# A decoder trunk on one core: the MLP up projection as its own stage with seven block products, its result through DRAM

## What is computed

```
for i in range(2):
    x = x + mixer_i(rmsnorm(x, norm_mix[i]))
    h = rmsnorm(x, norm_mlp[i])                       # (1024, 1024)
    x = x + square(relu(h @ w_up[i])) @ w_down[i]      # w_up (1024, 4096), w_down (4096, 1024)
```

## Time and profile before

| what | value |
|---|---|
| median of 3 runs | 2750.98 us (2746.82 to 2753.17) |
| the profiled execution | 2752.24 us, span of its trace 2750.4 us |
| PE busy | 2658.4 us (97%), 12273 matmuls |
| DVE busy | 1572.6 us (57%) |
| ACT busy | 746.5 us (27%) |
| POOL busy | 477.9 us (17%) |
| DMA | 146.67 MB, mean 53 GB/s |

### The profile page before, as it was taken

One profiled execution on the slowest core, in us unless ns is written; L12 is line 12 of the kernel. 1 busy time (PEld: TensorE's weight loads), 2 busy tenths in 40 slices (PEclk: granted clock), 3 DMA queues, 4 the chain that ended last, 5 costly groups with the idle time before them and its releaser, 6 DMA issues.

```text
span 2750.4 us, 35656 instructions
## 1 busy us (share of the span) xinstructions
PE 2658.4 (97%) x12273; PEld 2216.8 (81%) x12273; DVE 1572.6 (57%) x3049; ACT 746.5 (27%) x1400; POOL 477.9 (17%) x473
## 2 busy tenths in 40 slices
PE   8999999999999999999999988999979999999999
PEld 6878878788788788888888877888868888888887
DVE  7554454544677644544445488888875444454443
ACT  6232222322313211111111255555551111111112
POOL 2102011020001211111111153323331111111010
PEclk9999999999999999999999999999999999999999
DMA  6012120121432111111111101001011111111111
GB/s 201 27 47 69 47 74 12 47 65 51 149 97 87 39 54 46 46 46 48 59 46 46 38 23 39 17 24 39 32 31 46 46 46 60 46 46 46 46 46 61
DMA packets 124795, 146.67 MB, mean 53 GB/s; under 512 B 15729, under 2 KB 97937, under 8 KB 124690
## 3 DMA queue, kind: packets, MB, share of 16 engines
q1 hardware_dynamic: 122386, 141.14, 16.4%
q10 hardware_dynamic: 2304, 4.20, 0.4%
HBM read 128.54 MB, written 16.78 MB: 53 GB/s over the span
## 4 chain that ended last, share of the span: by engine, by line
PE 80%; DVE 11%; issue 5%; ACT 3%; POOL 0%; DVEq 0%; DMA 0%; ACTq 0%; SPq 0%; POOLq 0%
PE ps L420 26%; PE ps L422 26%; PE ps L421 25%; ACT xn L1460 1%; DVE xT L597 1%; DVE hT_lo L465 1%; DVE wqg_lo L387 1%; DVE smax L1507 1%; PE ps L858 1%; DVE pT_lo L1484 1%; PE ps L859 1%; PE ps L860 1%; DVE hss L1540 1%; PE ps L906 0%; PE ps L890 0%
## 5 line engine op out<-in xcount | busy, mean ns | idle before, releaser
L597 DVE TENSOR_TENSOR xT<-ps,xT 128x512 f32<-128x512 f32 x704 | 475.0, 689 | 273.7 <-PE ps L422 273.7
L420 PE MATMUL ps<-aT_hi,wd_hi 128*128 128x512 f32 x1408 | 555.2, 394 | 7.9 <-DVE xT L597 4.9
L421 PE MATMUL ps<-aT_lo,wd_hi 128*128 128x512 f32 x1408 | 550.3, 391 | 0.0
L422 PE MATMUL ps<-aT_hi,wd_lo 128*128 128x512 f32 x1408 | 550.2, 391 | 0.0
L420 PE MATMUL ps<-hT_hi,wu_hi 128*128 128x512 f32 x1024 | 401.1, 392 | 0.0
L422 PE MATMUL ps<-hT_hi,wu_lo 128*128 128x512 f32 x1024 | 399.1, 390 | 0.0
L421 PE MATMUL ps<-hT_lo,wu_hi 128*128 128x512 f32 x1024 | 399.1, 390 | 0.0
L694 POOL TENSOR_TENSOR sqr_t<-relu_t 128x512 f32<-128x512 f32 x128 | 188.1, 1470 | 1168.8 <-DVE relu_t L702 1168.8
L420 PEld LDWEIGHTS ps<-aT_hi,wd_hi 128*128 128x128 f32 x1408 | 265.8, 189 | 63.3 <-DVE xT L597 5.8
L422 PEld LDWEIGHTS ps<-aT_hi,wd_lo 128*128 128x128 f32 x1408 | 265.7, 189 | 55.9
L421 PEld LDWEIGHTS ps<-aT_lo,wd_hi 128*128 128x128 f32 x1408 | 266.0, 189 | 53.8
(11 more groups left out here) (255 smaller groups left out, 4333.4 us busy)
## 6 DMA issues: line engine op xcount, KB each, us to landing
raw<-in_w_up SPq DMA_DIRECT2D x64, 512.0 KB, 3.9
raw<-in_w_down SPq DMA_DIRECT2D x64, 512.0 KB, 3.3
raw<-in_ret_w_in SPq DMA_DIRECT2D x48, 512.0 KB, 4.7
y_dram<-xn SPq DMA_DIRECT2D x32, 256.0 KB, 2.3
raw<-y_dram SPq DMA_DIRECT2D x16, 512.0 KB, 3.2
raw<-in_ret_w_out SPq DMA_DIRECT2D x16, 512.0 KB, 3.4
xtok<-in_x SPq DMA_DIRECT2D x8, 512.0 KB, 5.9
xT<-x_dram SPq DMA_DIRECT2D x8, 512.0 KB, 7.5
```

The lines of the kernel that those rows point to most:

```text
L420: pe.matmul(bank, ah, bh, start=(i == 0), stop=False)
L421: pe.matmul(bank, ah, bl, start=False, stop=False)
L422: last = pe.matmul(bank, al, bh, start=False, stop=(i == len(pairs) - 1))
L597: dve.tensor_tensor(xT[:, k, cols], ps[:, banks[m % len(banks)], :], xT[:, k, cols], ALU.add).then_inc(x_add, 1)
```

## The change

The up projection is taken out of the groups. It becomes a stage of its own over 8 pairs of groups (512 hidden features each). In a pair the product is one of 2x2 blocks: the weights are split by the two halves of K and by two halves of the features, the activations by the two halves of K and the two halves of the tokens. Strassen's scheme in Winograd's form makes it of seven block products (numbered 1 to 7) in place of eight. With two feature tiles (q = 0, 1) a pair is 14 products of 4 x 3 = 12 matmuls, called steps 0 to 13 here. The seven activation operands `bh`/`bl` are made once a layer; the sums of weights (`u_sum`, 8 a pair) are made for each pair. Results are gathered in PSUM and in SBUF slots (`u_copy_act`, 6 a pair, and `u_add_dve`, 8 a pair), get their relu times `rb` (DVE, in place), their square (ACT, in place), and go to `a_dram` (8 stores of 256 KB). The first pair (`first=True`) has its own order of products, and its weight sums are POOL's. `xT` is saved to `x_dram` before the stage and read back at its end, since the operands take its room. The down projection then runs over the 16 groups as before, but reads `a` from DRAM in two pieces of 512 KB a group, split by ACT and DVE like weights. The norm before the MLP is done for both halves at once.

```diff
+ORDER = {True: (1, 2, 5, 6, 4, 7, 3), False: (1, 6, 4, 7, 2, 5, 3)}
+RESULTS = {True: ((11, 0), (11, 1), (22, 0), (21, 0), (22, 1), (21, 1), (12, 0), (12, 1)),
+           False: ((21, 0), (21, 1), (11, 0), (11, 1), (22, 0), (22, 1), (12, 0), (12, 1))}
+U_BANK = {1: 4, 6: 4, 7: 4, 2: 0, 5: 2, 3: 2, 4: 6}
...
+        def u_load_next(sp, layer, p, first):
+            g = PAIRS * layer + p
+            for j in range(4):
+                sp.wait_ge(u_lo, OPS * g + op_pos(first, 7 if j < 2 else 3, j % 2) + 1)
+                u_load(sp, layer, p + 1, j)
...
+        def u_sum(eng, layer, p, first, i, q):
+            g = PAIRS * layer + p
+            done = lambda k: eng.wait_ge(s_set, 8 * g + SUM_AT[first][k, q])
+            if i == 5:
+                arrived(eng, PC_U[layer], p, 4, q)
+                arrived(eng, PC_U[layer], p, 4, 2 + q)
+                wait(eng, u_lo, OPS * g)
+                eng.tensor_tensor(us1[:, q, :, :], weight(7, q), weight(4, q), ALU.add).then_inc(s_set, 1)
+            if i == 7:
+                done(5)
+                eng.tensor_tensor(weight(7, q), weight(1, q), weight(7, q), ALU.subtract).then_inc(s_set, 1)
+            if i == 6:
+                done(5)
+                wait(eng, s_set, 8 * g)
+                eng.tensor_tensor(us2[:, q, :, :], us1[:, q, :, :], weight(1, q), ALU.subtract).then_inc(s_set, 1)
...
+        def u_pe(pe, layer, p, first, between=lambda s: None):
+            for s in range(OPS):
...
+                if i == 6:
+                    pe.wait_ge(u_cp, 6 * g + 1 + q)
+                if i == 7:
+                    pe.wait_ge(u_cp, 6 * g + 3 + q)
+                if i == 3:
+                    pe.wait_ge(u_add, 8 * g + c_pos(first, 22, q) + 1)
+                product(pe, ps[:, U_BANK[i] + q, :],
...
                          bh[i][:, k, :], bl[i][:, k, :]) for k in range(4)], begin=i in (1, 2, 4, 5)).then_inc(u_mm, 1)
+                between(s)
...
+        def u_dve(dve, layer, p, ahead):
+            for s in range(OPS):
+                for c, q in results_of(s):
+                    u_add_dve(dve, layer, p, False, c, q)
+                if s + URING < OPS:
+                    if s + URING >= OPS - 2:
+                        u_sum(dve, layer, p, False, 3, s % 2 ^ 1)
+                    u_lo_dve(dve, layer, p, False, s + URING)
+                else:
+                    ahead(s)
+                for c, q in results_of(s):
+                    u_relu_dve(dve, layer, p, False, c, q)
...
+        def next_lo(dve, layer, p, s):
+            j = s + URING - OPS
+            if j in (2, 3):
+                for i in (5, 7, 6):
+                    u_sum(dve, layer, p + 1, False, i, j - 2)
+            u_lo_dve(dve, layer, p + 1, False, j)
...
+        def edge_dve(dve, layer, final):
+            for i in (0, 1):
+                u_lo_dve(dve, layer, 0, True, 4 + i)
+            for kk in range(4):
+                t_dve(dve, layer, 6, kk, final)
+            for kk in range(4):
+                b_lo_dve(dve, layer, 6, kk)
+            norm_rstd(dve, 2 * layer + 1, 0)
+            dve.wait_ge(n_rsq, RSQ * (RS_AT[2 * layer + 1] + 1))
+            for half in range(2):
+                norm_dg(dve, 2 * layer + 1, half)
+            (u_lo 6, 7; t_dve 4 x4; t_dve 7 x4; b_lo_dve 3 x4; b_lo_dve 4 x4; u_lo 8, 9; b_lo_dve 7 x4; u_lo 10, 11)
+            (u_add_dve 11 x2; u_relu_dve 11 x2; u_lo 12, 13)
+            for s in (7, 8, 9):
+                next_lo(dve, layer, 0, s)
+            for s in (10, 11):
+                for c in (22, 21):
+                    u_add_dve(dve, layer, 0, True, c, s - 10)
+                next_lo(dve, layer, 0, s)
+                for c in (22, 21):
+                    u_relu_dve(dve, layer, 0, True, c, s - 10)
...
+        def first_pair_pool(pool, layer, final):
+            pool.wait_ge(down_mm, final + TILES)
+            for q in range(2):
                u_sum(pool, layer, 0, True, 5, q)
            for q in range(2):
                u_sum(pool, layer, 0, True, 7, q)
                u_sum(pool, layer, 0, True, 6, q)
            for q in range(2):
                u_sum(pool, layer, 0, True, 3, q)
...
+            def between(s):
+                if s == 1:
+                    norm_stat_pe(pe, n, 0)
+                    pe.wait_ge(x_add, final + TILES)
+                if s == 3:
+                    for half in range(2):
+                        norm_rb_pe(pe, n, half)
...
+        def up_sp(sp, layer, final):
+            for m in range(TILES):
+                x_save(sp, m, final)
+            for c, q in RESULTS[True][:2]:
+                u_store(sp, layer, 0, True, c, q)
+            u_load_next(sp, layer, 0, True)
...
+            for kind in ("m1", "u2", "u3", "e"):
+                for q in range(2):
+                    sp.wait_ge(a_out[kind, q], 16 * PAIRS * (layer + 1))
...
+        def dn_dve(dve, layer, g, b):
+            for m in range(TILES):
+                if isinstance(g, int) and g == 0 and m < KT:
+                    dve.wait_ge(x_in_s[m], 16 * (3 + layer))
+                add(dve, DG_D[layer] + g, m)
+                if m % 4 == 0:
+                    dn_lo_dve(dve, layer, g + 1, m // 4, b)
```

More of the change, by code:

```diff
@@ L368, in load_piece @@
         def load_piece(sp, m0, i, per, j, src, fold):
-            wait(sp, w_lo, m0 + per * i + j - RING + 1)
+            wait(sp, w_lo, wc(m0) + per * i + j - RING + 1)
             apart(sp)
@@ new lines, in u_store, with weight @@
+        def u_store(sp, layer, p, first, c, q):
+            g = PAIRS * layer + p
+            kind = keep_of(first, c)
+            sp.wait_ge(u_sq, 8 * g + c_pos(first, c, q) + 1)
+            apart(sp)
+            half = c % 10 - 1
+            sp.dma_start(a_dram[bass.ds((4 * p + 2 * q + c // 10 - 1) * P, P), half * HALF:(half + 1) * HALF],
+                         keep(kind, q)).then_inc(a_out[kind, q], 16)
+        def weight(i, q):
+            k0 = raw[:, q, :].rearrange("p (k n) -> p k n", n=256)
+            k1 = raw[:, 2 + q, :].rearrange("p (k n) -> p k n", n=256)
+            return {1: k0[:, :, 0:P], 7: k0[:, :, P:2 * P], 2: k1[:, :, 0:P], 3: k1[:, :, 0:P], 4: k1[:, :, P:2 * P],
+                    5: us1[:, q, :, :], 6: us2[:, q, :, :]}[i]
@@ new lines, in u_hi_act @@
+        def u_hi_act(act, layer, p, first, s):
+            i, q = op_at(first, s)
+            g = PAIRS * layer + p
+            wait(act, u_mm, OPS * g + s - URING + 1)
+            if i in (1, 2, 4):
+                arrived(act, PC_U[layer], p, 4, q if i == 1 else 2 + q)
+            else:
+                act.wait_ge(s_set, 8 * g + SUM_AT[first][i, q])
+            if layer == 1 and first and s == 5:
+                act.wait_ge(n_ss, sums(3, 1, KT - 1))
+            act.activation(uw_hi[:, s % URING, :].rearrange("p (k n) -> p k n", n=P), weight(i, q),
+                           ACT.Copy).then_inc(u_hi, 1)
@@ new lines, in down_act @@
+        def down_act(act, layer, after):
+            for j in range(4):
+                dn_hi_act(act, layer, 1, j, 1)
+            after()
+            with act.Fori(1, MLP_GROUPS // 2) as gg:
+                for b in range(2):
+                    for j in range(4):
+                        dn_hi_act(act, layer, 2 * gg + b, j, D_BUF[b])
+        def dn_dve(dve, layer, g, b):
[5 more added lines that the diff above has]
+                    dn_lo_dve(dve, layer, g + 1, m // 4, b)
@@ new lines, in down_dve, with down_sp @@
+        def down_dve(dve, layer, last_adds):
+            dn_dve(dve, layer, 0, 1)
+            with dve.Fori(0, MLP_GROUPS // 2 - 1) as gg:
+                dn_dve(dve, layer, 2 * gg + 1, 2)
+                dn_dve(dve, layer, 2 * gg + 2, 1)
+            last_adds()
+        def down_sp(sp, layer):
+            for j in range(4):
+                dn_load(sp, layer, 1, j)
+            with sp.Fori(2, MLP_GROUPS) as g:
+                for j in range(4):
+                    dn_load(sp, layer, g, j)
```

963 lines of the change are left out of this document (610 added, 353 removed).

## The result

The changed kernel took 2784.41 us (median of four runs, 2783.64 to 2784.62) against 2752.07 us (2746.82 to 2753.94) for the kernel before on the same chip: a ratio of 1.0119, 95% interval 1.0103 to 1.0135. It is slower by 32 us; the forecast was 2752, the range 2716 to 2776. The profiled run's span is 2781.6 us against 2750.4.

A forecast was written before the change was run, and what follows sets the result against it. It took TensorE (97% busy) and its matmul count as the bound. From a profiled 2752.24 us, -87.0 + 27.6 + 46.1 + 11.6 + 2.4 = +0.7 us; adjusted to the median, it forecast 2752, range 2716 to 2776.

The forecast's parts named there:

- saving of 87 us: Up projections of both layers: 384 fewer matmuls at 0.2267 us each, 87.0 us less if TensorE stays as dense.
- Steady pairs: Pairs 1 to 6, both layers: DVE's three sums in each of steps 9 and 10 cost 2.3 us a pair, 27.6 us.
- Last pair: Pair 7 of each layer: no sums for a next pair, so 0 lost.
- Edge, layer 0: Into layer 0's up projection and through its first pair: gaps at statistics, rb products and step 12 cost 25.0 us more.
- Edge, layer 1: Same chain at layer 1, its first gap gone as TensorE is busy until 2042.1: 21.1 us more.
- Up to down: First down group: wait of 4.1 us for DVE plus a clock fall of 1.7, 5.8 a layer, 11.6 us.
- Attention: Weight splits come later on DVE, ahead of the norm for which TensorE waits: 2.4 us, bounds 0 and 5.
- rb gap: First pair, ahead of `norm_rb_pe`: 10.8 us waiting for DVE, slowed by POOL's sums at 1.04 us each.
- Loads: End of layer 0's first pair: loads issued after result 11's stores delay DVE's adds; 7.6 us gap before step 12.
- Clock: Behind each longer gap the clock falls to 1.2 GHz for 3.4 us, losing 1.7 us; none after 1.94 us.
- Steady pairs keep up: Rival for the middle pairs: DVE's mean load of 23 us in 38 fits, no 27.6 loss; 2724 us, chance 0.24.
- Each gap of the steady pairs also drops the clock: Rival: one clock fall in each of 12 middle pairs, 20.4 us more; 2772 us, chance 0.22.

The follow-up runs named there:

- The edit that breaks it: Changed kernel with ACT making b5's high part ahead of b3's high part and the square in tiles 12 to 15: 2775.03 us.
- the filling: Changed kernel with unread matmuls on PE ahead of the statistics (layer 0), the rb products and step 12 of the first pairs: 2788.45 us.
- setting them aside: Changed kernel with DVE's low parts behind the step's relu in the middle pairs' steps 0 to 8, sums left in place: 2770.84 us.
- POOL's sums: Changed kernel with six of POOL's eight weight sums in each layer's first pair given to DVE: 2775.53 us.
- spread sums: Changed kernel with the middle pairs' six next-pair sums spread over steps 8 to 11 and low parts behind the relu: 2743.97 us.

## Why the prediction was wrong

The saving of 87 us was right, and so were most of the places at which PE would wait: each middle pair, the three gaps of the first pairs, the first down group. The sum failed by its losses, nearly all sized too small: the two edges by 12.5 us of the 30.3 that it is off, up to down by 6.7, the steady pairs by 5.4, the last pair by 4.9. Two of them, layer 1's drain and the last pair, it put at nothing. By the prediction's own terms, each less what the kernel before lost at the same place (8.2 and 4.6 us at the two edges):

| Term | predicted | measured |
|---|---|---|
| Steady pairs | 12 x 2.3 = 27.6 | 12 x 2.75 = 33.0 |
| Last pair | 0 | 4.4 + 0.5 = 4.9 |
| Edge, layer 0 | 25.0 | 36.9 - 8.2 = 28.7 |
| Edge, layer 1 | 21.1 | 7.4 + 27.1 - 4.6 = 29.9 |
| Up to down | 11.6 | 8.8 + 9.5 = 18.3 |
| Attention | 2.4 | 0.9 + 2.7 = 3.6 |
| Tail | 0 | -0.4 |

They sum to 118.0 in place of 87.7. Less the 87.0 these are 31.0 us, and the span grew by 31.2.

- **The step that failed most, the edge.** "16 x 0.60 + 20 x 0.65 + 1.5 of waits for tiles 0 to 2", giving 906.0 for the last one, is DVE's work without its waits behind tile 2. DVE ended at 912.5. In tiles 12 to 15 the low part of b5 waits for a high part that needs nothing new, but stands in ACT's list behind two steps that need DVE's add of the same tile: 1.83 us a tile, a handoff there and back. The edit that breaks it took 5 us off layer 0's gap and 3.8 off layer 1's. Layer 1 was predicted without a gap ahead of its first product; in its drain, the attention's last group, 7.4 us more were lost than before, 3.8 of them this. The rest of it, where only two banks alternate, was not tried. The prediction names 1.22 us of waiting at this edge of the kernel before; PE's timeline before has a longer wait just ahead of it, in the drain, and the 7.4 us come on top of that:

```profile
2034.96 0.76 PE L420 MATMUL ps<-aT_hi,wd_hi 128*128 128x512 f32 x1 [4.70 <-DVE xT L597]
```

- **rb gap.** Predicted 10.8 us, measured 7.4: PE had been held longer at the statistics, so less of the wait for the same list was left for here. Contention was right in size, 1.04 us per POOL addition by the t6 rows. The rule of the Trainium skill (SBUF — State Buffer, "Who interferes with whom") agrees with them.
- **Loads.** The chain ahead of steps 12 and 13 came as told, by its mechanism and its size: predicted 7.6 and (from its 965.1) some 1.5 us, measured 6.6 and 1.45 in layer 0.
- **Clock.** I counted 1.7 us behind each long gap, from one fall of 3.4 us. At gaps of 5 to 9 us the falls lasted 6.8 to 13.7 us, from within the gap on, and in the first pair of layer 0 the part that PE worked through cost 8.5 us in place of 5.1. But where the filling took a fall away, PE waited for DVE instead, so those 8.5 are no term of their own. A fall is shown to cost its own time where PE was the bound behind it: up to down (2.3 and 2.6 us) and on step 13 of the filled kernel (1.7). The two falls in layer 1's drain were not tried. I had added gap and fall at every place.
- **Up to down.** The mechanism was right (the first low part of the next group, with the adds behind it), the gap mis-sized: predicted 4.1, measured 6.4 and 6.9, and the falls 2.3 and 2.6 in place of 1.7. Later low parts removed the falls and all but 1.6 and 0.8 us of the gaps.
- **Attention.** That 2.7 is near 2.4 is luck. At the attention's start, where the wait was predicted, layer 0's last down group lost 0.9 us more and the first heads 0.65 less than before; the rest, 3.4 us, came in the middle of the attention, where no wait was predicted. The net 2.7 is 1.5 to 3.7 us in the changed kernel and its variants, and its cause stays open.
- **Steady pairs.** DVE's two steps with sums take 4.52 us each, predicted 4.56. It enters them later than the 0.5 us I took, for the waits of 0.62 to 0.70 us in steps 6 to 8 add up; setting them aside gave 0.7 us a pair.
- **Last pair.** "Pair 7 has no next sums: 0" left out what it has: the first group's splits of 1.23 us, with 1.05 us of waiting for ACT ahead of each, and in layer 0 the attention's tables. Layer 1, without the tables, lost 0.5 us, layer 0 4.4.
- **The rivals.** "Steady pairs keep up" is false for this order of the sums and true for another: 38.08 us. "Each gap of the steady pairs also drops the clock" is false: the clock is 1.00 in the windows of all twelve, with gaps of 0.8 and 1.66 us in each.

One thing was wrong throughout. From the start of the first up projection to the end of the span, the edits that undo one loss each gave 9.1 (b5), 3.9 (POOL's sums), 16.7 (up to down) and 34.3 us (spread sums), 64.0 together, and the kernel with all of them and a reordered first pair gave 78.2. In it the middle pairs from the third on (38.08) and the first down groups (22.7 and 22.6 us against 23.6 and 22.6) are as with each edit alone. There the losses stood side by side, so errors of one sign added up, where my range let them offset one another; within the first two pairs, where the reordering is in it too, this is not shown.

## What to carry to other kernels

An engine at 66% load was the bound at nearly every edge here: write its list with each wait and what stands between an instruction and the one that it waits for on the other engine, for a sum of durations misses handoffs there and back. Spread extra work so that no two consecutive steps exceed the pace of the engine that matters, and put what another engine waits for ahead of it. A gap is worth its length only if nothing behind it is bound by the same list; where the same list decides the next wait too, moving the gap gave 0 to 2 us of 7 here.

## What the runs showed of the hardware

- A fall of the granted clock to 0.50 (1.2 GHz) lasted 3.4 us at the gap of 2.4 us ahead of step 12 of layer 0's last pair, and 6.8 to 13.7 us at gaps of 5 to 9 us, where it began within the gap. At the gaps of 0.8 and 1.66 us of the middle pairs none came. With matmuls that nobody reads in the gaps four of five falls did not come, two others came later, and the time did not get better.
- Four DVE instructions with two inputs in SBUF took 6.87 us beside four POOL additions and 2.73 us without them. Six sums a layer moved from POOL to DVE made each first pair 1.8 to 2.5 us shorter, though they are 3.7 us more of work for DVE.
